# Layer 0's gates, head sums and first waits reordered; in layer 1 the keys' norm chain set ahead of the memory maxima

## The reference, cut to what matters

```
# layer 0
qk, v, o, ig, fg, mq = split(rms_norm(h) @ w_in)
qk = silu(causal_conv(qk))
h_tilde = mlstm(q, k, v, ig + b_i, log_sigmoid(fg + b_f))      # 4 heads of 192
main = rms_norm(h_tilde, h_norm) * sigmoid(o)
y_mem = memory_attention(mq, mem_k, mem_v)                     # 4 heads of 64
h = h + concat(main, y_mem) @ w_out ;  h = h + swiglu(rms_norm(h))
# layer 1
c_q, c_kv, k_r, mq = split(rms_norm(h) @ w_in)
q, k = rope(rms_norm(c_q @ w_uq)), rope(rms_norm([c_kv @ w_ukv, k_r]))   # 6 heads of 192
main = causal_softmax_attention(q, k, v)
h = h + concat(main, memory_attention(mq, mem_k, mem_v)) @ w_out
h = h + top-2-of-8 experts(rms_norm(h))
```

## Time and profile before

| what | us |
|---|---|
| median of three runs | 1505.06 (1502.91 to 1505.12) |
| the profiled execution, device time | 1504.15 |
| its span | 1502.3 |
| PE busy | 1452.8 (97%) |
| DVE busy | 1204.8 (80%) |
| ACT busy | 1056.8 (70%) |
| span up to the end of layer 0's mixer | about 161 |
| layer 1's mixer | about 403 to 516 |

### The profile page before, as it was taken

One profiled execution on the slowest core, in us unless ns is written; L12 is line 12 of the kernel. 1 busy time (PEld: TensorE's weight loads), 2 busy tenths in 40 slices (PEclk: granted clock), 3 DMA queues, 4 the chain that ended last, 5 costly groups with the idle time before them and its releaser, 6 DMA issues.

```text
span 1502.3 us, 22103 instructions
## 1 busy us (share of the span) xinstructions
PE 1452.8 (97%) x7008; PEld 1217.8 (81%) x7008; DVE 1204.8 (80%) x1569; ACT 1056.8 (70%) x1399; POOL 37.4 (2%) x86
## 2 busy tenths in 40 slices
PE   6998999999998999999999999999999999999995
PEld 5987888888886788888888888888888888888884
DVE  5966665554665589999989989899999999999994
ACT  5664644444485478887888888888888878888783
POOL 1000000000000000000000000000000000000000
PEclk9999999999998999999999999999999999999998
DMA  7553465555251569999999999999999999999991
GB/s 255 180 180 122 144 225 192 171 192 185 72 183 57 189 241 391 382 362 396 375 361 393 382 358 394 381 371 379 387 381 363 391 378 365 393 378 361 393 396 69
DMA packets 192107, 442.03 MB, mean 294 GB/s; under 512 B 8798, under 2 KB 20412, under 8 KB 192060
## 3 DMA queue, kind: packets, MB, share of 16 engines
q1 hardware_dynamic: 188940, 429.90, 78.7%
q0 software_dynamic: 3120, 11.54, 2.7%
HBM read 433.54 MB, written 7.86 MB: 294 GB/s over the span
## 4 chain that ended last, share of the span: by engine, by line
PE 93%; DVE 3%; ACT 2%; issue 1%; DMA 0%; SPq 0%; DVEq 0%; ACTq 0%
PE bank L477 89%; PE bank L1038 1%; DVE w_lo L1674 0%; PE bank L1017 0%; DVE xT_lo L1716 0%; PE bank L763 0%; PE bank L489 0%; DMA late<-in_mem_dram 0%; PE bank L668 0%; PE bank L1045 0%; ACT w_hi L1177 0%; ACT scr L1514 0%; ACT kT L1478 0%; ACT scr L1462 0%; DVE msmall L1834 0%
## 5 line engine op out<-in xcount | busy, mean ns | idle before, releaser
L1674 DVE TENSOR_TENSOR w_lo<-raw,w_hi 128x1024 fp32r<-128x1024 f32 (+1 forms) x832 | 955.6, 1198 | 160.0 <-ACT w_hi L1177 148.6
L1177 ACT ACTIVATE w_hi<-raw 128x1024 fp32r<-128x1024 f32 (+1 forms) x832 | 841.3, 1043 | 211.9 <-PE bank L477 202.8
L477 PE MATMUL bank<-w_hi,xT_hi 128*128 128x512 f32 (+4 forms) x1358 | 529.0, 390 | 10.3 <-issue 3.4
L477 PE MATMUL bank<-w_hi,xT_lo 128*128 128x512 f32 (+4 forms) x1358 | 521.9, 384 | 0.0
L477 PE MATMUL bank<-w_lo,xT_hi 128*128 128x512 f32 (+4 forms) x1358 | 521.2, 384 | 0.0
L477 PEld LDWEIGHTS bank<-w_hi,xT_hi 128*128 128x128 f32 x1358 | 255.9, 188 | 58.6 <-issue 7.8
L477 PEld LDWEIGHTS bank<-w_hi,xT_lo 128*128 128x128 f32 x1358 | 255.6, 188 | 49.5
L477 PEld LDWEIGHTS bank<-w_lo,xT_hi 128*128 128x128 f32 x1358 | 256.1, 189 | 46.5
L477 PE MATMUL bank<-w_hi,aT_hi 128*128 128x512 f32 x544 | 212.6, 391 | 0.7 <-DVE aT_lo L2390 0.7
L477 PE MATMUL bank<-w_hi,aT_lo 128*128 128x512 f32 x544 | 211.8, 389 | 0.0
L477 PE MATMUL bank<-w_lo,aT_hi 128*128 128x512 f32 x544 | 211.7, 389 | 0.0
(11 more groups left out here) (361 smaller groups left out, 744.9 us busy)
## 6 DMA issues: line engine op xcount, KB each, us to landing
raw<-in_we_gate_dram SPq DMA_DIRECT2D x112, 1024.0 KB, 7.2
raw<-in_we_up_dram SPq DMA_DIRECT2D x112, 1024.0 KB, 7.5
raw<-in_we_down_dram SPq DMA_DIRECT2D x112, 1024.0 KB, 6.9
raw<-in_w_gate_dram SPq DMA_DIRECT2D x14, 1024.0 KB, 5.0
raw<-in_w_up_dram SPq DMA_DIRECT2D x14, 1024.0 KB, 5.0
raw<-in_w_down_dram SPq DMA_DIRECT2D x14, 1024.0 KB, 4.9
raw<-in_w_in_dram SPq DMA_DIRECT2D x16, 768.0 KB, 4.8
raw<-in_w_out_dram SPq DMA_DIRECT2D x8, 1024.0 KB, 5.2
```

Of the source, the lines that this page charges most:

```text
L477: return pe.matmul(o, a, b, start=start, stop=stop, skip_group_check=True, **kw)
L1177: act.activation(split_piece(w_hi, c, shape, half), raw_piece(c, shape, half), ACT.Copy).then_inc(hi_ready, 1)
L1674: dve.tensor_tensor(split_piece(w_lo, c, shape, half), raw_piece(c, shape, half), F(split_piece(w_hi, c, shape, half)), ALU.subtract).then ...
```

## The change

*Layer 0, early (DVE).* The splits of the two pieces of the q/k tile's second chunk stand ahead of the norm chain of the memory keys instead of behind it.

The diff, cut to its core (the arguments that only pass `late` and `behind_first` on are left out):

```diff
@@ columns, inside the loop over the pieces @@
                         last.then_inc(piece_used, 1)
+                        if behind_first and (j, half) == (0, 0):
+                            behind_first()
+                        if late and j == 1 and half == 0:
+                            late()
@@ PE, layer 0 @@
             def mem_scores(layer, kmTs):
+                pe.wait_ge(sem("qk_copied"), 4)
                 pe.wait_ge(sem("mem_ops_ready"), layer + 1)
...
             def head_sums():
 
+                pe.wait_ge(sem("tile_evacuated"), 3)
                 for hd in range(LH):
...
             pe.wait_ge(sem("decay_exp"), LH)
-            pe.wait_ge(sem("qk_copied"), 4)
             proj(full(C_V, 384), 384, between=lambda: mem_scores(0, kmTs_0))
...
             mem_sums(0, pmT_0)
-            proj(full(C_V + 4, 384), 384, between=head_scores)
-            pe.wait_ge(sem("tile_evacuated"), 3)
-            head_sums()
-            proj(full(C_V + 6, 384), 384)
-
-            pe.wait_ge(sem("y_ready"), 1)
-            transpose_rows(lambda t, k: y[:, t, k * P:(k + 1) * P], KD)
+            proj(full(C_V + 4, 384), 384, between=head_scores, late=head_sums)
+            proj(full(C_V + 6, 384), 384, rows_first=True)
+
+            transpose_rows(lambda t, k: y[:, t, k * P:(k + 1) * P], KD, after=("y_ready", 0))
@@ PE, layer 1 @@
-            keep_busy(50, 5)
+            keep_busy(22, 5)
...
             pair_turned(rotk, 1, B[4][:, S:2 * S]).then_inc(sem("headsT_psum"), 1)
-            mem_turned(1)
             pe.wait_ge(sem("headsT_ready"), 6)
...
             scores(1)
+            mem_turned(1)
+            scores(2)
             mem_sums(1, pmT_1)
-            scores(2)
             probs_turned(0)
...
             values(3)
-            proj(full(C_OUT1, 512), 512, ready=22, between=last_heads, turn_order=(2, 3, 4, 1))
+            values(4)
+            probs_turned(5)
+            proj(full(C_OUT1, 512), 512, ready=22, turn_order=(2, 3, 4, 1), behind_first=lambda: values(5))
@@ ACT, layer 0 @@
             def gates_out(t):
 
-                whole(C_V + 4 + 2 * t + 2)
+                if t == 0:
+                    whole(C_V + 6)
                 for tb in range(TB):
+                    if t == 1 and tb == 0:
+                        act.wait_ge(sem("first_rows"), 1)
+                    if t == 1 and tb == 1:
+                        whole(C_V + 8)
                     ins = act.activation(og[:, tb, 384 * t:384 * t + 384], tile_bank(3 + t, tb)[:, 0:384], ACT.Sigmoid)
-                ins.then_inc(sem("tile_evacuated"), 1)
+                    ins.then_inc(sem("tile_evacuated" if tb else "gate_first"), 1)
...
             act.wait_ge(sem("mem_out_psum"), 1)
-            gates_out(0)
-            splits_to(2 * C_OUT0 + 1)
-
+            splits_to(2 * C_OUT0)
             act.wait_ge(sem("mnum_psum"), LH)
...
                 ins.then_inc(sem("head_sumsq"), 1)
+            gates_out(0)
             splits_to(2 * C_OUT0 + 3)
             gates_out(1)
@@ ACT, layer 1 @@
-            mem_exps(1)
+            act.activation(small[:, 63:64], iota[:, 0:1], ACT.Exp)
...
             turned(krT[:, 2, :], B[5][:, 0:S], 10)
-            mem_turned(1, pmT_1)
-            splits_to(2 * C_OUT1 + 1)
+            mem_exps(1)
+
...
             probs_exp(0)
+            mem_turned(1, pmT_1)
             probs_exp(1)
+            splits_to(2 * C_OUT1)
             probs_exp(2)
             probs_turned(0)
-            splits_to(2 * C_OUT1 + 2)
+            splits_to(2 * C_OUT1 + 1)
             probs_exp(3)
             high_T(2, 22, None, bank0=3, k0=6)
             probs_turned(1)
-            splits_to(2 * C_OUT1 + 3)
+            splits_to(2 * C_OUT1 + 2)
...
-            splits_to(2 * C_OUT1 + 5)
+            splits_to(2 * C_OUT1 + 3)
             probs_turned(5)
+            splits_to(2 * C_OUT1 + 4)
@@ DVE, layer 0 @@
+            splits_to(2 * C_QK + 3)
             variance(16, MD)
             rsqrt(16)
...
-            splits_to(2 * C_QK + 3)
...
-            gate_gain(0)
-            splits_to(2 * C_OUT0 + 1)
...
-            heads_out(0)
-            gate_gain(1)
+            for hd in range(LH):
+                for t in range(TB):
+                    c = t * LH + hd
+                    step(dve.scalar_tensor_tensor(out=y[:, t, hd * LD:(hd + 1) * LD], in0=B[hd][:, t * S:t * S + LD],
+                                                  scalar=small[:, 24 + c:25 + c], in1=hnorm_bc[:, :], op0=ALU.mult,
+                                                  op1=ALU.mult))
             settle()
-            heads_out(1)
-            splits_to(2 * C_OUT0 + 3)
+
+            def gated(half, t):
+                if t:
+                    dve.wait_ge(sem("tile_evacuated"), 4 + half)
+                else:
+                    dve.wait_ge(sem("gate_first"), half + 1)
+                cols = slice(384 * half, 384 * half + 384)
+                return dve.tensor_tensor(y[:, t, cols], y[:, t, cols], og[:, t, cols], ALU.mult)
+
+            for t in range(TB):
+                step(gated(0, t))
+            splits_to(2 * C_OUT0)
+            settle()
+            for t in range(TB):
+                gated(1, t).then_inc(sem("y_ready"), 1)
+            splits_to(2 * C_OUT0 + 1)
             low_T(KD, 8, None)
@@ DVE, layer 1 @@
-            mem_max(1)
...
                 sem("k_ready"), 1)
-            splits_to(2 * C_OUT1 + 1)
+            mem_max(1)
...
             probs_scaled(0)
+            softmax(2)
+            splits_to(2 * C_OUT1)
             mem_out(1)
-            softmax(2)
             probs_scaled(1)
-            splits_to(2 * C_OUT1 + 2)
+            splits_to(2 * C_OUT1 + 1)
             softmax(3)
             probs_scaled(2)
             low_T(2, 22, None, bank0=3, k0=6)
-            splits_to(2 * C_OUT1 + 3)
+            splits_to(2 * C_OUT1 + 2)
...
-            splits_to(2 * C_OUT1 + 5)
+            splits_to(2 * C_OUT1 + 3)
+            splits_to(2 * C_OUT1 + 4)
```

28 lines of the change are left out of this document (5 added, 23 removed).

## The result

| | before | with the change |
|---|---|---|
| median, us | 1505.09 (1502.91 to 1505.68, 4 executions) | 1490.70 (1489.82 to 1491.09, 4 executions) |
| profiled execution, us | 1504.15 | 1490.69 |
| its span, us | 1502.3 | 1488.9 |

The changed kernel takes 0.9904 of the time of before, with a 95% interval of 0.9892 to 0.9917. That is 14.4 us less in the medians and 13.4 us less in the two profiled spans; the interval goes from 12.5 to 16.3 us, so the trace's 13.4 lies inside it and the forecast's sum of 11.45 does not. The forecast was 1493.2 us with a range of 1490.0 to 1497.5.

What follows compares the result with a forecast made beforehand. PE was taken to bound the kernel (93% of the chain), so gains ahead of the experts arrive in full. 0.6 + 2.1 + 1.95 + 6.8 = 11.45 us gave 1492.7, or 1493.6 by the median; forecast 1493.2, range 1490.0 to 1497.5.

Steps and rivals of the forecast that it cites:

- Layer 0, early splits: Splits ahead of the memory keys' norm chain: PE's 1.73 us gap goes, a later wait remains; gain 0.6 us.
- Layer 0, the values: Eviction wait moved into `mem_scores`: half a tile of matmuls covers PE's 2.10 us idle before the values; gain 2.1 us.
- rival of the moved wait that comes back: A moved wait returns in full in `mem_scores` and the early split gains nothing: 1495.4 us, chance 0.06.
- Layer 0, gates and heads: End of layer 0's mixer: earlier head sums and squares start the output projection sooner; gain 1.95 us.
- The rival of the gates that hold: Layer 0's end gives nothing, as DVE's gate steps and heads precede the transposes: 1494.7 us, chance 0.08.
- Layer 1, keys: Keys' norm chain ahead of the maxima, 22 idle transposes: keys' transposes 3.6 us earlier, first scores at 453.6 against 458.44.
- a clock below 1.00 before the first scores: Layer 1: a granted clock under full before head 0's scores would make the prediction wrong.
- the slower rival: Shorter `keep_busy` drops the clock before layer 1's first scores until the projection: 13 to 19 us more, 1508.7, chance 0.04.
- Layer 1, heads: Layer 1's heads: splits leave DVE's path, memory exponentials go to ACT; softmax 3 comes 5.1 us earlier.
- that rival (13%): Memory exponentials and copies on ACT hold up layer 1's heads, leaving only the keys' 3.6 us: 1495.9 us, chance 0.13.
- Last heads and projection: Layer 1: last heads and a quarter of the projection run without PE waits, the longer 1.54 us before; gain 1.7 us.
- the rival without a fall: Layer 1's last heads bunch so the clock stays up: gain there 9.2 us, 1490.3 us, chance 0.07.

Runs made afterwards that it cites:

- the edit alone: Kernel before with only layer 0's gates, head sums and squares edits (squares ahead of sigmoids, gates behind heads): 1501.91 us, ratio 0.9997.
- The run with the old place: Changed kernel with the last heads back in the middle of layer 1's output projection and one ACT split moved back: 1491.92 us, ratio 0.9932.
- session 1: First follow-up session, on its own chip: kernel before 1505.98 us, parts of the change alone, and the changed kernel again unedited at 1490.42 us, ratio 0.9899.
- session 3: Third follow-up session, on another chip: kernel before 1502.90 us, with four edited kernels from 1487.06 to 1502.64 us.
- layer 0's first two edits alone: Kernel before with only the early splits and the last q/k eviction wait moved into the memory scores: 1502.29 us, ratio 0.9980.

## Why the prediction was right, and where it was short

**Layer 0, early splits: right.** PE's gap is 1.18, forecast 1.2, and the next tile starts 0.57 us earlier (49.20 against 49.77), forecast 0.6.

**Layer 0, the values: right.** No wait takes the place of the 2.10 us. Both edits together were to give 2.7 us; the trace has 2.74, and their own run 3.0, between 1.5 and 4.7. The rival of the moved wait that comes back falls.

**Layer 0, gates and heads: right.** The term was 1.95; the whole change shows 1.88 (58.62 us less 56.74), the edit alone 1.8 in its trace; its timing doesn't tell it from nothing. The rival of the gates that hold falls.

**Layer 1, keys: right, with 0.5 us less than forecast.** The chain ends at 445.45, forecast 450.0 less 4.65, or 445.35. The step that failed is the end of the idle transposes: 450.4 less 4.65 is 445.75, and they ended at 446.40. They started 0.7 late, since the clock had fallen at 434 and the 28 transposes ahead of them took 4.55 in place of 3.22 us. That fall is not the change's doing: three kernels with the old layer 1 have it in their traces too. First scores: 4.3 us of layer 1's own, forecast 4.8. By its wording one of my signs of being wrong came up here, a clock below 1.00 before the first scores. It was not the fall that the slower rival meant, which would have stood behind `keep_busy` and run into the scores; there the clock was at 1.00. But the sign was badly drawn, and so was "falls once, late among the heads": the trace has four falls, two of them in layer 0, where the kernel before has them too.

**Layer 1, heads: right.** The fifth head's probabilities come 4.8 us earlier by layer 1's edits, forecast 5.1. The memory exponentials take 4.3 us on ACT (forecast 4.5) and the copies 2.12 (forecast 2), and neither holds the heads; that rival (13%) falls.

**Last heads and projection: mis-sized.** The term was 1.7 us; it measured 2.66 (29.80 less 27.14). The run with the old place brings 2.16 of it back, and the rest by an estimate of the clock's part. I had counted the wait of 1.54 and a little more, and left out the second wait, 0.58 in that run; for the last 0.5 the traces show no single wait. The time at half clock behind the probabilities, set equal in both, was equal (5.1 and 5.0 us). Its cost I had put at 2.5; in the changed kernel, filling the waits gave 1.9. So the rival without a fall, which did not come, was priced 0.5 too high.

**Routing: missing from the sum.** I had let nothing change behind the projection. Before, the clock fell at 525, and the gather of the first expert's rows ran into it; the two lines are from before and after:

```profile
525.19 5.47 PE L477 MATMUL bank<-onehot,h 128*128 128x128 f32 x32 [0.30 <-DVE onehot L2228]
```

```profile
513.13 3.84 PE L477 MATMUL bank<-onehot,h 128*128 128x128 f32 x32 [0.31 <-DVE onehot L2234]
```

That is 1.6 us, and 1.5 of it reach the first expert matmul. It goes with layer 1's version in most traces, though not in all: of the five traces with the old layer 1, four have the fall at the gather; of the nine with the new one, one has it, the changed kernel's own second trace. Why it comes more seldom behind the new projection is open.

**The sum.** 11.45, plus 0.96 for the last heads, plus 1.5 for the gather, less 0.3 for the keys and heads and 0.03 for layer 0, is the 13.5 us at the first expert matmul. The medians have 1 us more (14.4), and session 1 has 15.2. Which falls make up that last microsecond stays open, but it goes with the clock. In session 1 the seventeen executions of before lay in two groups: six at 1501.9 to 1502.9 us with a mean granted clock of 0.987 to 0.991, and eleven at 1505.0 to 1507.8 with 0.985 to 0.987, and the median fell into the second. In session 3, 17 of 21 lay below 1504.2. One source of such spread is in the traces: the clock falls at 21 to 24 us in 6 of the 13 traces that left that wait unfilled, and where it does not, what follows comes some 1.6 us earlier, counted from the first weight tile. That is in kernels of either kind, and does not favour the change. Which falls the long executions have more of can't be said, since only one execution of each kernel was profiled, two of the changed one.

**The slower rival.** It did not come. Its price was some three times too high, as the run without `keep_busy` shows: 4.7 us by the trace in an execution with the fall, 2.7 to 3.0 in the median. The step that was wrong is that nothing in the heads lifts the clock again: it was back at 460, when PE had run for 11 us without a wait. The Trainium skill ("TensorE: Matmul & The Clock Gate", section on HAM oscillation) says that a gap between bursts makes the next burst start cold. That run's trace agrees, with 2.46 us of waiting ahead of the fall at 446; but the two short executions of the same kernel, whose mean clock was 0.991, speak for a gap that does not do it every time.

## What to carry to other kernels

Ask of every wait on a shared chain which input ends last, and put first the chain whose input is there first: the keys' chain had its input before the maxima had theirs (6.8 and 8.2 us behind the last key and value tile in the kernel before, 6.9 and 8.8 where the clock fell at 434), and they take 2.6 us. When a chain gets shorter, shorten the idle work that had been cut to its length, or it becomes the new bound (3.1 us here); without any, the next burst can start at half clock. And walk forward from one instruction that both kernels have, piece by piece, to the first stretch that is surely alike in both: the one piece that I didn't walk, the routing, held most of the error in the trace.

## What the runs showed of the hardware

**What a fall costs depends on whether PE had a wait to give.** Where PE ran without one, 10.93 us at half clock did the work of 5.98. Behind the fall at 434, 28 transposes took 1.33 us longer (4.55 in place of 3.22) and the first scores came only 0.7 later: a wait of 0.77 us for ACT had gone. Behind the one at 475, 5.0 us at half clock cost 1.9.

**Neither a wait nor its length says by itself whether the clock falls.** The wait ahead of the first weight tile was 2.99 us in the changed kernel, with a fall behind it, and 2.98 with layer 0's first two edits alone, without one. The fall at 61 stands in ten of fourteen traces, and PE waits nowhere near it: with layer 0's edits alone it was busy for all 6.00 us from 59 to 65, at a mean clock of 0.72.

**The clock also comes back while PE runs nothing but idle transposes:** in the changed kernel's trace they run from 434.50 to 438.9, and the clock is back at 437.2.

**Where the clock falls changes between executions of one kernel.** The changed kernel's two traces share the falls at 21, 62, 434 and 475; one has another at 512 and the other has none there. The Trainium skill ("TensorE: Matmul & The Clock Gate", section on the HAM clock gate) says of the warm-up at a kernel's start that it varies from run to run; the traces here show as much for falls in the middle of a kernel. A difference of 1 to 1.6 us between two single profiles can be this alone, so a term of that size needs a count over several traces.

**Idle transposes in waits that PE has anyway kept the clock at 1.00 in the traces:** 1.9 us for the fall at 475, 0.7 for the one at 434, by one trace each; the ratios don't show either. At the gap ahead of the transposes of `y` they gave nothing that the timing could tell: two of the three traces with that gap unfilled have a fall there, and it cost 0.7 to 0.8 us.
